# A fused two-layer transformer kernel: who computes the first layer's short convolution, and when three loads and one product are issued

## The reference

```python
# first block: the state-space branch begins with a causal convolution of four taps over tokens, per channel
xbc = jax.nn.silu(causal_dwconv(xbc, conv_w, conv_b))      # 3072 channels, conv_w (4, 3072)
dt = jax.nn.softplus(dt_raw + dt_bias)                     # 32 heads

# first block: the feed-forward's second product
u = causal_dwconv(h @ w_up, dw_w, dw_b)                    # three taps
gate, val = jnp.split(u, 2, axis=-1)
ffn = (jax.nn.silu(gate) * val) @ w_down                   # 2816 -> 1024

# second block: the conditioning vector c gives shifts, scales and gates, needed only there
mod = jax.nn.silu(c) @ w_ada + b_ada                       # 1024 -> 6144
```

## Time and profile before

| | us |
|---|---|
| median of 3 runs | 1343.15 (1341.98 to 1345.96) |
| the profiled execution's own time | 1343.3 |
| its span, first to last instruction | 1341.4 |
| TensorE busy | 1293.9 (96%) |
| VectorE busy | 804.1 (60%) |
| ScalarE busy | 306.9 (23%) |
| GpSimd busy | 51.8 (4%) |

### The profile page before, as it was taken

The page is one execution under the profiler, slowest core; times in us unless marked ns, Lnnn a source line. Parts: engine busy times, 40 slices in busy tenths (PEclk is TensorE's granted clock), DMA queues, the critical chain, the costliest instruction groups (busy, mean ns, idle before and its releaser), DMA issues.

```text
span 1341.4 us, 20533 instructions
## 1 busy us (share of the span) xinstructions
PE 1293.9 (96%) x8023; PEld 932.5 (70%) x8038; DVE 804.1 (60%) x1671; ACT 306.9 (23%) x647; POOL 51.8 (4%) x60
## 2 busy tenths in 40 slices
PE   8998899999999999999899999999999999999997
PEld 6887788888889999999695888844333433343332
DVE  5686568999775999777668786244323332332322
ACT  2311123221202322300343432034111211112112
POOL 0000311200000011100000000000000000000001
PEclk9999899999999999999999999999999999999999
DMA  9768333343695645356335139669999999999995
GB/s 367 296 250 298 128 124 125 125 144 126 218 369 161 193 151 189 83 135 232 126 127 188 64 137 365 251 244 360 414 425 427 427 428 427 429 426 427 426 421 220
DMA packets 123724, 351.16 MB, mean 262 GB/s; under 512 B 4848, under 2 KB 66544, under 8 KB 110320
## 3 DMA queue, kind: packets, MB, share of 16 engines
q1 hardware_dynamic: 122016, 348.68, 68.1%
q10 hardware_dynamic: 1616, 1.20, 0.3%
HBM read 348.82 MB, written 1.05 MB: 261 GB/s over the span
## 4 chain that ended last, share of the span: by engine, by line
PE 72%; DVE 15%; DMA 6%; issue 3%; ACT 2%; DVEq 1%; POOL 0%; POOLq 0%; ACTq 0%
PE bank L1495 22%; PE bank L933 19%; PE bank L1231 9%; PE bank L985 6%; DMA arena<-in_w_gate 5%; PE bank L1463 3%; PE bank L1585 3%; DVE arena L2227 2%; PE bank L1247 2%; PE bank L1311 2%; DVE arena L2159 2%; DVE arena L2146 1%; DMA wdt<-in_w_in 1%; DVE scratch L2241 1%; PE bank L1005 1%
## 5 line engine op out<-in xcount | busy, mean ns | idle before, releaser
L933 PE MATMUL bank<-hT,dense 128*128 128x256 f32 x1152 | 254.3, 382 | 2.5 <-DMA dense<-in_w_in 1.7
L933 PEld LDWEIGHTS bank<-hT,dense 128*128 128x128 f32 x1152 | 218.8, 191 | 36.7 <-issue 4.9
L1495 PE MATMUL bank<-arena,scratch 128*64 128x512 f32 x768 | 189.0, 596 | 4.0 <-DMA arena<-in_w_gate 4.0
L933 PE MATMUL bank<-arena,dense 128*128 128x256 f32 x704 | 153.7, 380 | 0.4 <-DVE arena L2303 0.4
L933 PEld LDWEIGHTS bank<-arena,dense 128*128 128x128 f32 x704 | 133.3, 190 | 20.0 <-issue 2.0
L1495 PEld LDWEIGHTS bank<-arena,scratch 128*64 128x64 f32 x768 | 59.4, 137 | 101.2 <-issue 93.5
L1495 PE MATMUL bank<-arena,hT 128*64 128x512 f32 x416 | 113.4, 595 | 0.7 <-ACT hT L1998 0.7
L2227 DVE SCALAR_TENSOR_TENSOR arena<-arena,par 128x256 f32<-128x256 f32 x240 | 97.8, 486 | 0.0
L2891 DVE TENSOR_TENSOR scratch<-scratch,bank 128x512 f32<-128x512 f32 x64 | 41.2, 684 | 91.9 <-PE bank L1585 90.5
L2909 DVE SCALAR_TENSOR_TENSOR resid<-bank,lamp,resid 128x512 f32<-128x512 f32 x32 | 24.0, 750 | 94.3 <-PE bank L1495 94.3
L1495 PEld LDWEIGHTS bank<-arena,hT 128*64 128x64 f32 x416 | 34.7, 137 | 62.3 <-issue 60.0
(11 more groups left out here) (434 smaller groups left out, 1844.6 us busy)
## 6 DMA issues: line engine op xcount, KB each, us to landing
arena<-in_w_down SPq DMA_DIRECT2D x22, 2048.0 KB, 25.3
arena<-in_w_gate SPq DMA_DIRECT2D x21, 2048.0 KB, 22.9
dense<-in_w_in SPq DMA_DIRECT2D x17, 2048.0 KB, 8.6
arena<-in_w_up SPq DMA_DIRECT2D x15, 2048.0 KB, 23.0
arena<-in_w_ada SPq DMA_DIRECT2D x12, 2048.0 KB, 10.4
dense<-in_w_up SPq DMA_DIRECT2D x10, 2048.0 KB, 21.5
arena<-in_w_up SPq DMA_DIRECT2D x14, 1024.0 KB, 23.4
dense<-in_w_ffn_up SPq DMA_DIRECT2D x12, 1024.0 KB, 7.5
```

The source lines that it names most:

```text
L933: last = mm(dst, chunk(k, m), src[:, k, :], start=k == 0, stop=k == k_n - 1)
L1495: last = mm(dst[e * CAP:(e + 1) * CAP, :], tokens(k, e), w[e][k], start=k == 0, stop=k == k_n - 1)
```

## The change

1. ScalarE does the first of the four taps (a copy with a scale, out of PSUM) and counts `first_taps`. VectorE does the other three, alternating between the two channel groups, so that an operation waits for the one two before it. VectorE's and ScalarE's loops are written out. The silu of a tile stands behind the first tap of the next.
2. Row transfers go behind the units: 0 and 1 behind unit 2 instead of unit 1, row transfer 2 behind unit 3, and so on; each glu unit now stands in front of a row transfer.
3. Row sums 0 and 1 stand behind VectorE's dt steps; row sums 6 and 7 behind glu products 1 and 2.
4. The first product of down tile 1 is done right behind that of tile 0.
5. At the end of the up product, ScalarE does the first taps of tile 21 before the silu of tile 20, and VectorE's last repair moves ahead of the first activation difference.

```diff
+            summed_with = {("xbc", 2): (0, 1), ("xbc", 3): (2,), ("xbc", 4): (3,), ("xbc", 5): (4,), ("glu", 0): (5,),
+                           ("glu", 1): (6,), ("glu", 2): (7,), ("glu", 3): (8,)}
             for u in range(6):
                 load("xbc", u, flat, wi[:, :, u * 512 + C_XBC:(u + 1) * 512 + C_XBC])
                 if u == 1:
                     sp.dma_start(c_act, c_rows).then_inc(sem_("c_in"), 16)
-                    load_ada(0)
-                    load_ada(1)
-                elif u > 1:
-                    load_ada(u)
+                for i in summed_with.get(("xbc", u), ()):
+                    load_ada(i)
             for u in range(4):
                 load("glu", u, halves, wglu2[:, :, :, u * 256:(u + 1) * 256])
-                if u < 3:
-                    load_ada(6 + u)
+                for i in summed_with["glu", u]:
+                    load_ada(i)
...
+                begin(sem_("act_ready"), DK)
+                if t != 1:
+                    raw_product(t)
+                if t == 0:
+                    raw_product(1)
                 if t:
                     have("down", t - 1)
-                begin(sem_("act_ready"), DK)
-                product(first[:, 0, :], r1[:, 0:DK, :], lo[:, :, TOK[0]])
...
+            def xbc_taps(t):
+                b = wait_tile(act, "xbc", t)
+                for m in range(2):
+                    j = 2 * t + m
+                    f(xbcT[:, j, :], b[:, m * T:(m + 1) * T], ACT.Copy, scale=par("ssm_w", j * 4 + 3, 1)
+                      ).then_inc(sem_("first_taps"), 1)
...
+            for t in range(3):
+                xbc_silu(t)
+            for t in range(4, 12):
+                xbc_taps(t)
+                xbc_silu(t - 1)
+            xbc_silu(11)
...
+            first_taps(19)
+            silu_gate(19)
+            first_taps(20)
+            first_taps(21)
+            silu_gate(20)
+            silu_gate(21)
...
+            def xbc_conv(t):
+                b = bank[TILE["xbc", t] % NB]
+                dve.wait_ge(sem_("first_taps"), 2 * t + 2)
+                for tap in range(1, 4):
                     for m in range(2):
+                        j = 2 * t + m
+                        if tap > 1:
+                            own.wait(1)
+                        own.add(stt(xbcT[:, j, tap:T], b[:, m * T:m * T + T - tap], par("ssm_w", j * 4 + (3 - tap), 1),
+                                    xbcT[:, j, tap:T], ALU.mult, ALU.add))
+                own.wait()
+                dve.sem_inc(read_sem("xbc", t), 1)
...
+            dve.wait_ge(sem_("x_std"), TT + 1)
+            ada_sum(0)
+            ada_sum(1)
+            for t in range(4, 12):
+                xbc_conv(t)
+                if t % 2:
+                    ada_sum(t // 2)
...
             for t in range(4):
                 glu(t)
-                if t % 2:
-                    ada_sum(6 + t // 2)
+                if t in (1, 2):
+                    ada_sum(5 + t)
...
             fix_third("up", NFAST_UP - 2)
+            fix_third("up", NFAST_UP - 1)
             act_sum(0)
-            fix_third("up", NFAST_UP - 1)
```

More of the change, by code:

```diff
@@ L1237, in down_products @@
             def down_products(t):
-                first, second, third = (v3(b[:], P) for b in (open_tile("down", t), *down_bank[t]))
+                first, second, third = (v3(b[:], P) for b in (bank[TILE["down", t] % NB], *down_bank[t]))
                 (r1, r2), (s1, s2, s4), (t1, t2, t3, t4) = down_raw[t], down_sums[t], act_sums
@@ L1252, in begin, with raw_product @@
                         pe.wait_ge(sem_of, n)
-                if t != 2:
-                    pe.wait_ge(down_arrival[t], 32 if t == 0 else 16)
+                def raw_product(t):
+                    if t != 2:
+                        pe.wait_ge(down_arrival[t], 32 if t == 0 else 16)
+                    else:
+                        have("down", 1)
+                    product(v3(open_tile("down", t)[:], P)[:, 0, :], down_raw[t][0][:, 0:DK, :], lo[:, :, TOK[0]])
+                begin(sem_("act_ready"), DK)
[3 more added lines that the diff above has]
+                    raw_product(1)
                 if t:
                     have("down", t - 1)
-                begin(sem_("act_ready"), DK)
-                product(first[:, 0, :], r1[:, 0:DK, :], lo[:, :, TOK[0]])
                 pe.wait_ge(sem_("down_summed"), 4 * t + 1)
@@ L1698, in _, with xbc_silu @@
             f(c_act, c_act, ACT.Silu).then_inc(sem_("x_std"), 1)
+            def xbc_taps(t):
[4 more added lines that the diff above has]
+                      ).then_inc(sem_("first_taps"), 1)
+            def xbc_silu(t):
+                wait_read(act, TILE["xbc", t])
+                for m in range(2):
+                    j = 2 * t + m
+                    f(xbcT[:, j, :], xbcT[:, j, :], ACT.Silu, bias=par("ssm_b", j, 1)).then_inc(sem_("xbc_ready"), 1)
+            act.wait_ge(params_in, 16)
+            xbc_taps(0)
             act.wait_ge(sem_("rows_done"), 4)
             f(dt_rows, bank[6][:, 0:T], ACT.Copy).then_inc(sem_("rows_copied"), 1)
-            act.wait_ge(params_in, 16)
+            for t in range(1, 4):
+                xbc_taps(t)
             act.wait_ge(sem_("x_var"), TT + 2)
@@ L2138, in _, with ada_sum @@
                         ins.then_inc(read_sem("h", t), 1)
-            def ada_sum(i, turn=0):
-                dve.wait_ge(sem_(f"ada_in{i % 2}"), turn * 16 + (i // 2 + 1) * 16)
+            def ada_sum(i):
+                dve.wait_ge(sem_(f"ada_in{i % 2}"), 16 * (i // 2 + 1))
                 w = v3(ada_slot[i % 2], D)
@@ L2146, in ada_sum @@
                     stt(w[:, m, :], w[:, m, :], 1.0, c_act, ALU.mult, ALU.mult,
[L2147 to L2152, removed]
-                    for m in range(2):
[L2154 to L2164, removed]
-                    if t % 2:
-                        if t == 1 and first:
-                            dve.wait_ge(sem_("x_std"), TT + 1)
-                        ada_sum(t // 2, i)
+                        accum_out=mod[:, 4 * i + m:4 * i + m + 1]).then_inc(sem_("ada_summed"), 1)
+            def xbc_conv(t):
+                b = bank[TILE["xbc", t] % NB]
+                dve.wait_ge(sem_("first_taps"), 2 * t + 2)
+                for tap in range(1, 4):
+                    for m in range(2):
+                        j = 2 * t + m
+                        if tap > 1:
[4 more added lines that the diff above has]
+                dve.sem_inc(read_sem("xbc", t), 1)
             dve.wait_ge(params_in, 16)
-            xbc_tiles(0, first=True)
+            for t in range(4):
+                xbc_conv(t)
             dve.wait_ge(sem_("dt_done"), 1)
```

8 lines of the change are left out of this document (2 added, 6 removed).

## The result

The changed kernel takes 1328.9 us (median of 4 runs, 1326.71 to 1330.12); the kernel before took 1344.56 beside it (4 runs). The ratio is 0.9884 (95% interval 0.9861 to 0.9906), so 12.6 to 18.7 us are gone. The forecast was 1330.0 and a sum of 13.2. The profiled execution is the fastest of the four: 1326.71 us, with a span of 1324.9, which is 16.5 less than the span before.

A forecast was written before the change was run, and what follows sets the result against it. TensorE, working through nearly the whole span, was taken to set the time, so only its gaps could be won back. Terms of 2.27 + 1.6 + 4.96 + 1.1 + 3.26 = 13.2 us gave 1330 us, range 1326 to 1337.

The forecast's parts named there:

- A: TensorE's wait for the small dt weights (wdt) ahead of L1044 goes: 2.27 us, bounds 0 and 2.27.
- B: TensorE's waits for input weight units (1.37 and 0.36 us) go, 0.1 charged for unit 4: 1.6 us, bounds 0.5 and 1.7.
- C: The fourth gap, TensorE's wait for VectorE at L1064, goes with the slow unit behind it: 4.96 us, lower bound 3.4.
- D: At the token-major transposes L1075, 1.1 of the 4.44 us gap goes; the wait changes from row sum to its transfer.
- the rows could have come before glu unit 2's data: Rival at the transposes, 10%: row transfer 7 lands with or before the unit; D is 4.6, time 1326.6 us.
- E: At the first down tile, TensorE's four products run without a wait: 3.26 us, lower bound 1.3.
- no wait is left at L1064: Against the rival, 5%, that VectorE is still late at L1064: C goes and the time is 1335 us.
- none at the down tile: Against the rival, 12%, that the down tile keeps its wait: E is near 0, time 1333.3 us.
- none for unit 4: Against the rival, 3%, of a slower kernel: unit 4 waits behind a late row sum 0; at 72 us, time 1347.
- TensorE's longest wait from 145 to 460 us is still 0.4: Against the rival, 5%, that the gain is given back in later waits: only E stays, 1340 us.

The follow-up runs named there:

- the experiment that undoes it: The kernel after, with row transfers 0 and 1 again behind unit 1, in front of unit 2: 1332.71 us, one run.
- the chained version: The kernel after, with all four taps on VectorE, one channel group after the other, each operation waiting for the one before, no loop: 1329.61 us, one run.
- the second profile: The kernel after run once more, unchanged: 1329.51 us, span 1327.7, one run.
- the runs of two other kernels: Kernel before with only down tile 1's first product moved: 1343.6 us; kernel after with row transfers 0 and 1 in front of unit 2: 1332.71 us.

## Why the prediction was right

The time (1328.9 for 1330.0) and the mechanisms came out, with some luck in the time: the sum was 13.2 and the measured difference 15.7, but the kernel before ran 1.4 us slower beside the changed one (1344.56) than in the runs that the forecast started from (1343.15). The terms, each against its measurement:

A, forecast 2.27. L1044 starts 28.14 - 25.90 = 2.24 us earlier and waits for nothing. Right, and the experiment that undoes it brings the wait back. The argument there, half of the traffic gone so wdt in time, left room to spare: wdt came 7.7 us earlier where 2.3 were needed.

B, forecast 1.6. From L1044 to glu unit 0 it is 2.16 us less: the waits of 1.37 and 0.36, and 0.43 more. The term was right in kind and too small. Unit 4 did fit: row sum 0 ended at 54.2, forecast 54.7, and there is no wait at 68.7. The 0.43 is what two gaps cost beside the idle time in their brackets. A unit's row lasts 14.08 us, but when nothing is waited for the next row starts before that end: in an unbroken row a unit takes 55.42 / 4 = 13.86 us. In front of a gap this overlap is missing, so each gap removed gives 0.2 more.

C, forecast 4.96. The wait at L1064 and the slow unit are gone: glu unit 0 and the gap take 3.56 us less (17.46 before, 110.78 - 96.88 = 13.90 after), the next unit 15.51 - 13.81 = 1.70 less, 5.26 together, with the same 0.2 and 0.1 over the sum. The diagnosis, idle time inside a hardware loop, is what the chained version shows. But the prediction's price of a pair, 12 x 0.50 + 4.65, took ScalarE's tap into account, as if VectorE kept up by it. It was not needed: with sixteen operations at 0.50 a pair costs 12.65 us, still below TensorE's 13.9, and the chained version waits only 0.26. The alternation, which the prediction gave no price, was not needed either.

D, forecast 1.1, measured 0.2. This is the term that was furthest off. VectorE turned to the transposes at 130.10, forecast 130.1, from the landing of row transfer 7 at 125.18, forecast 125.2. But TensorE began them at 124.70, not 125.6, since B and C gave 0.9 more than forecast. The distance is 130.10 - 124.70 = 5.40, against 5.61 before. What counts is VectorE's own shift, 140.02 - 130.10 = 9.92, and the forecast for it, A + B + C + D = 9.93, was met. That it was met so closely is luck, as SP's queue shows:

```profile
110.97 1.25 SPq L587 DMA_DIRECT2D dense<-in_w_in  x2
112.27 1.29 SPq L611 DMA_DIRECT2D arena<-in_w_ada  x1
```

TensorE ended glu unit 0 at 110.78, 0.7 us earlier than the forecast 111.5. The row transfer was issued 1.5 us behind that end, not 0.4, and landed 12.9 us after its issue, not 13.3: 14.4 us in place of 13.7. The two errors cancel. The transfer's issue hangs on that end, so a us that TensorE gains ahead of it moves the transfer too: in the run with row transfers 0 and 1 in front, L1064 comes 3.89 us later and VectorE's turn 4.00. Only what TensorE gains behind it, in glu unit 1, is waited for again at the transposes. The wait changed from the row sum to its transfer, as forecast, and moving that transfer removes all of it but 0.89.

The rule weighed there, the Trainium skill, DMA: Bandwidth & Descriptors, section Queues, rings and completion order, says that completion is not FIFO per issuing engine. By it the rows could have come before glu unit 2's data. They did not: row transfer 7, issued behind that unit, took 12.9 us, and the unit's halves 6.9 (median of the two). What brought the rows in time was issuing them earlier.

E, forecast 3.26, measured 3.23. GpSimd's last product, before and then in the change:

```profile
577.16 0.72 POOL L878 TENSOR_TENSOR region<-scratch 128x256 f32<-128x256 f32 x1 [2.48 <-ACT scratch L1807]
...
564.63 0.72 POOL L878 TENSOR_TENSOR region<-scratch 128x256 f32<-128x256 f32 x1 [1.16 <-ACT scratch L1825]
```

It stands 564.63 - 556.69 = 7.94 us behind the first raw product, against 577.16 - 567.66 = 9.50 before: 1.56 earlier, where I had taken about 1.0. It is there at 565.35, and TensorE's last two matmuls of L1273 need it at about 566.3 (564.06 + 20/22 x 2.46).

What the sum did not hold. The shift grows from 9.92 on VectorE to 10.97 at the first raw product, then to 14.20, then by 1.69 at L1005 (3.72 us after, and before the row below), and by 0.6 behind it, to 16.5.

```profile
643.40 5.41 PE L1005 MATMUL bank<-scratch,con 128*128 128x256 f32 x16 [1.90 <-ACT scratch L1843]
```

The first step of 1.0 and the 1.69 are the two stretches in which two executions of the same kernel differ by 0.98 and 1.69. So they can be had or lost without any edit. Against the second profile the span is 1341.4 - 1327.7 = 13.7 us shorter, and 13.2 was the forecast; the median difference, 15.7, lies between the two profiles' 13.7 and 16.5, and its interval holds both. The 0.6 stands beside waits for expert weights of 6.0 us before and 4.9 after; no experiment separates it, and over all ten traces the stretch from the start of L985 to the end takes between 681.2 and 683.4 us.

The rivals fell: no wait is left at L1064, none at the down tile, none for unit 4, and TensorE's longest wait from 145 to 460 us is still 0.4. The gain reached the end.

## What to carry to other kernels

A wait has a neighbour: before crediting a shift, ask which event the next wait is tied to, and move that event too; here one transfer issued earlier was worth 4.8 us more than the whole change, by the medians. Look for what an engine loses between its instructions before giving its work to another engine: with the loop written out, VectorE did all its taps itself and the gap of 3.37 us shrank to 0.26. And compare two profiles of one kernel before explaining a difference of 1 to 3 us by an edit.

## What the runs showed of the hardware that was not expected

- Dependent VectorE operations of 128x255 and 128x256 had 0.03 us of idle time each in front of them written out (2.0 us over 64), and 0.19 in a hardware loop (12.1 over 64, 0.5 of it a wait for TensorE). Whether the loop's own instructions, its waits on a counted value or its addresses by the counter make the difference was not tried.
- Two independent chains taken in turn need 0.405 us an operation (6 in 2.43), though one lasts 0.474; a single chain in written-out code needs 0.50 (8 in 4.02).
- Behind a wait of about 2 us TensorE's matmuls come back at full speed in one execution and partly at the lower clock in another, at the same place of the same kernel. The price was 1.69 us at L1005 (granted clock 1.00 and 0.74). Behind the wait for wdt it was nothing before (1.00) and about 1.65 in the runs of two other kernels (0.90). The Trainium skill, TensorE: Matmul & The Clock Gate, Part 1, says that the window by which the clock is set runs free and that the same kernel therefore shows another number of slow matmuls at its start from run to run. The two profiles of the kernel after, 3.72 and 5.41 us, agree in kind, though in the middle of the kernel; no run here shows that the cause is the same.
